# Eight units on the input without its root, in three places of a two-layer transformer trunk

## The reference, cut to what is computed

```python
def _rms(x, g):
    xf = x.astype(jnp.float32)
    y = xf * lax.rsqrt(jnp.mean(xf * xf, axis=-1, keepdims=True) + EPS)
    return (y * g.astype(jnp.float32)).astype(x.dtype)
...
def _layer(x, cond, p, lam_init, pos, ctx):
    mod = jnp.einsum('bd,de->be', jax.nn.silu(cond), p['w_ada']) + p['b_ada']
    sh1, sc1, g1, sh2, sc2, g2 = jnp.split(mod[:, None, :], 6, axis=-1)
    h = _rms(x, p['g_norm1']) * (1 + sc1) + sh1
    u = h @ p['w_in']
    gates, xa, qkv_da, xc, mla_in = jnp.split(u, IN_SPLITS, axis=-1)
    ...
    merged = jnp.sum(gsig * proj, axis=2)
    x = x + g1 * (merged @ p['w_out'])
    h2 = _rms(x, p['g_norm2']) * (1 + sc2) + sh2
    x = x + g2 * _conv_ffn(h2, p['w_up'], p['conv_w'], p['conv_b'], p['w_down'])
```

## Time and profile before

| | |
|---|---|
| three runs | 1223.28, 1224.08, 1226.67 us, median 1224.08 |
| profiled execution, its own time | 1223.51 us |
| its span, first to last instruction | 1221.7 us |
| PE busy | 99 % of the span, 7816 matmuls |
| DVE busy | 74 % |
| ACT busy | 47 % |
| POOL busy | 11 % |
| chain that ended last | PE 93 %, DVE 2 %, POOL 2 %, DMA 1 %, issue 1 % |

### The profile page before, as it was taken

How to read it: one execution, slowest core, us unless ns; L and a number is a source line. 1 busy time by engine, 2 the same in 40 slices (tenths; PEclk the granted TensorE clock), 3 DMA queues, 4 the chain that set the end, 5 groups by cost and what they waited for, 6 DMA issues and landing times.

```text
span 1221.7 us, 19781 instructions
## 1 busy us (share of the span) xinstructions
PE 1208.0 (99%) x7816; PEld 1149.7 (94%) x7816; DVE 901.4 (74%) x1671; ACT 575.6 (47%) x949; POOL 136.8 (11%) x109
## 2 busy tenths in 40 slices
PE   8999999999999999999999999999999999999998
PEld 7987999989989999999989889999998999999998
DVE  5597877748689999986876965765686887887432
ACT  3445564643365544532354455645425554454321
POOL 0232000008300000000202500000271000000000
PEclk9999999999999999999999999999999999999999
DMA  9763433444744444469664522332345334334443
GB/s 370 291 220 125 147 117 112 172 139 161 253 173 144 167 156 159 169 216 322 214 234 163 189 87 87 104 104 87 104 167 196 122 124 135 122 123 136 134 142 121
DMA packets 53532, 198.82 MB, mean 163 GB/s; under 512 B 6784, under 2 KB 7200, under 8 KB 51904
## 3 DMA queue, kind: packets, MB, share of 16 engines
q1 hardware_dynamic: 53120, 196.86, 46.0%
q0 software_dynamic: 320, 0.69, 0.2%
HBM read 195.25 MB, written 2.27 MB: 162 GB/s over the span
## 4 chain that ended last, share of the span: by engine, by line
PE 93%; DVE 2%; POOL 2%; DMA 1%; issue 1%; ACT 0%; SPq 0%; DVEq 0%; POOLq 0%; ACTq 0%
PE bank L1444 27%; PE bank L1446 27%; PE bank L1445 26%; PE bank L1743 1%; PE bank L1723 1%; PE bank L1512 1%; DVE w_lo L980 1%; DMA start_ada<-start_ada 1%; PE bank L1517 1%; PE bank L1516 1%; POOL wide L653 1%; PE bank L1713 1%; POOL merge_sum L655 1%; PE bank L1501 1%; PE bank L1698 1%
## 5 line engine op out<-in xcount | busy, mean ns | idle before, releaser
L1444 PE MATMUL bank<-act_hi,w_hi 128*128 128x384 f32 x1368 | 465.0, 340 | 0.7 <-DVE act_lo L1055 0.3
L1446 PE MATMUL bank<-act_hi,w_lo 128*128 128x384 f32 x1368 | 457.8, 335 | 0.0
L1445 PE MATMUL bank<-act_lo,w_hi 128*128 128x384 f32 x1336 | 446.6, 334 | 0.0
L980 DVE TENSOR_TENSOR w_lo<-w_raw,w_hi 128x1024 fp32r<-128x1024 f32 x251 | 318.9, 1272 | 114.6 <-ACT w_hi L662 113.6
L662 ACT ACTIVATE w_hi<-w_raw 128x1024 fp32r<-128x1024 f32 x251 | 264.3, 1054 | 167.8 <-DMA w_raw<-stream 167.7
L1444 PEld LDWEIGHTS bank<-act_hi,w_hi 128*128 128x128 f32 x1368 | 257.1, 188 | 10.7 <-issue 6.5
L1446 PEld LDWEIGHTS bank<-act_hi,w_lo 128*128 128x128 f32 x1368 | 256.8, 188 | 0.0
L1445 PEld LDWEIGHTS bank<-act_lo,w_hi 128*128 128x128 f32 x1336 | 251.0, 188 | 0.6
L1446 PE MATMUL bank<-mlp_hi,w_lo 128*128 128x384 f32 x352 | 118.3, 336 | 0.0
L1444 PE MATMUL bank<-mlp_hi,w_hi 128*128 128x384 f32 x352 | 118.3, 336 | 0.0
L1445 PE MATMUL bank<-mlp_lo,w_hi 128*128 128x384 f32 x352 | 118.3, 336 | 0.0
(11 more groups left out here) (246 smaller groups left out, 1576.0 us busy)
## 6 DMA issues: line engine op xcount, KB each, us to landing
w_raw<-stream SPq DMA_DIRECT2D x251, 512.0 KB, 3.3
ada<-ada_rows SPq DMA_DIRECT2D x48, 512.0 KB, 4.4
start_ada<-start_ada SPq DMA_DIRECT2D x8, 1024.0 KB, 17.9
ada_norm<-ada_w SPq DMA_DIRECT2D x16, 512.0 KB, 5.8
ada<-ada_w SPq DMA_DIRECT2D x8, 512.0 KB, 5.5
start_raw<-start_w SPq DMA_DIRECT2D x8, 448.0 KB, 18.5
ada_head_a<-ada_w SPq DMA_DIRECT2D x5, 512.0 KB, 7.3
cond_spread_mix<-cond_rows SPq DMA_DIRECT2D x2, 1024.0 KB, 7.9
```

What stands on the lines that cost most here:

```text
L980: V.tensor_tensor(wlo[s][:, :], raw[s][:, :], whi[s][:, :].bitcast(F32), ALU.subtract).then_inc(lo_ready, 1)
L1444: T.matmul(out, wb[s][0][:, w, :], hi[k], start=first and k == 0, stop=False)
L1445: T.matmul(out, wb[s][0][:, w, :], lo[k], start=False, stop=False)
L1446: ins = T.matmul(out, wb[s][1][:, w, :], hi[k], start=False, stop=last and k == n - 1)
```

## The change

It does three things of one kind, and moves what they displace.

1. **Start (layer 0).** The seven units and an eighth are multiplied with x·scale, without the root; two more columns carry the shift of the two conditionings, so the matmuls have 386 columns. Behind the products DVE multiplies each bank by the root (`start_rescale`) and ACT adds the shift's product (`start_add_shift`). The root is made in the middle of the loop (`roots(0)` at j = 4). The normalised x, which the later units need, is made meanwhile: POOL x·scale·root, ACT plus shift, DVE the low rest, at the blocks that `START_NORMED` names. x is loaded in four quarters between the weights, the modulation weights have three buffers (six before), and PE's warm-up has 6 products (11 before).
2. **Second mixing stage (layer 1).** `first_units(0, ...)`: units 0 to 7 on the unnormalised x, 386 columns, the sum of squares between blocks 4 and 5 of the first unit. ACT and DVE prepare the unnormalised high and low part during the down stage of layer 0.
3. **Second up stage (layer 1).** The same with `first_units(1, ...)`: the first eight up units go to eight banks, are rescaled in place, and then pass the convolution.

`hole_units` and the second `norm_units` are gone with their loads; the modulation vectors (1,3) and (1,5) are made by DVE's row products instead: layer 1 has the `MIX_ROWS` and `STEP_ROWS` of layer 0 (32 products where there were 16), and 16 more from the fourth group of four up units on (`SLOW_ROWS`). In the down stage of layer 0 the 26 row products lie at other units (`DOWN_ROWS`) and read a vector loaded anew (`spread_down`, 1 MB). The mixing units change order: xc0 and xc1 before k0 and k1.

The diff, cut:

```diff
-START_ADA = 6
-WARM = 11
+START_ADA = 3
+WARM = 6
+START_UNITS = SKIP + 1
+START_NORMED = {4: (0,), 5: (1, 2), 6: (3, 4), 7: (5, 6)}
...
+FIRST = 8
+SLOW_ROWS = 3
...
@@ POOL @@
+                def normed(n):
+                    pool.wait_ge(rstd_ready, l * 2 + n + 1)
+                    for k in range(KD):
+                        nc.gpsimd.tensor_tensor(wide[:, k, :], late[:, k, :], rsn, ALU.mult).then_inc(norm_full, 1)
...
+                    pool.wait_ge(rstd_ready, 1)
+                    for k in range(KD):
+                        pool.wait_ge(start_full, k + 1)
+                        nc.gpsimd.tensor_tensor(wide[:, k, :], late[:, k, :], rsn, ALU.mult).then_inc(norm_full, 1)
...
@@ ACT @@
+                def unnormed_high(n, d):
+                    for a, e, c in RANGES:
+                        ins = A(late[:, d, a:e], x[:, d, a:e], ACT.Copy, scale=(sc1, sc2)[n][:, d, c:c + 1])
+                    ins.then_inc(u_full, 1)
+                    act.wait_ge(u_full, n * KD + d + 1)
+                    A(uhi[n][:, d, 0:TOK], late[:, d, :], ACT.Copy).then_inc(u_hi, 1)
...
                 if l == 0:
-                    for u in range(SKIP, SKIP + 3):
-                        split(u)
+                    for j in range(KD):
+                        if j < KD // 2:
+                            start_square(j)
+                        start_high(j)
+                        if j == KD // 2:
+                            roots(0)
+                        start_unnormed_high(j)
+                        for k in START_NORMED.get(j, ()):
+                            normed_high(0, k)
+                    split(SKIP)
+                    normed_high(0, KD - 1)
+                    split(SKIP + 1)
+                    for q in range(START_UNITS):
+                        start_add_shift(q)
+                        if q == 2:
+                            split(SKIP + 2)
+                        if MIX[q] in SQUARED:
+                            mix_squares(q)
...
@@ DVE @@
+                def rescale(n, q, out):
+                    u = (0, P0)[n] + q
+                    dve.wait_ge(rstd_ready, l * 2 + n + 1)
+                    dve.wait_ge(unit_done, FROM + l * UNITS + u + 1)
+                    b = bank[q % (4, 8)[n]]
+                    V.tensor_copy(sums_shift[:, q, :], b[:, TOK:wide_w])
+                    V.tensor_tensor(out, b[:, 0:TOK], rsn, ALU.mult).then_inc(rescaled, 1)
...
+                    start_low(j)
+                    dve.wait_ge(start_u_hi, j + 1)
+                    low(sulo[:, j, 0:TOK], late[:, j, :], suhi[:, j, 0:TOK])
+                    low(sulo[:, j, TOK:start_width], mod[:, j, :], suhi[:, j, TOK:start_width]).then_inc(start_u_lo, 1)
...
                     for j in range(KD):
-                        start_norm(j)
-                    for u in range(SKIP, SKIP + 3):
-                        split(u)
+                        start_unnormed_low(j)
+                        for k in START_NORMED.get(j, ()):
+                            normed_low(0, k)
+                    split(SKIP)
+                    normed_low(0, KD - 1)
+                    split(SKIP + 1)
+                    for q in range(START_UNITS):
+                        start_rescale(q)
+                        if q == 2:
+                            split(SKIP + 2)
...
@@ DVE, up pairs @@
+                        unnormed = l > 0 and i < 2
+                        first, b0 = 3 * (2 * i + j), up_bank(i, 2 * j)
+                        if unnormed and p > l * FB:
+                            split(u + 4, i)
+                        elif not unnormed and (l == 0 or i > 2 or j > 0):
+                            split(u + 3, i)
...
+                        if unnormed and first < KD:
+                            normed_low(1, first)
                         dve.wait_ge(mlp_tanh, p + 1)
...
+                        if unnormed and first + 1 < KD:
+                            normed_low(1, first + 1)
+                        split(u + (5 if unnormed else 4), i)
+                        if unnormed and b0 < FIRST - 2:
+                            rescale(1, b0 + 2, bank[b0 + 2][:, 0:TOK])
...
+                        if unnormed and b0 < FIRST - 2:
+                            rescale(1, b0 + 3, bank[b0 + 3][:, 0:TOK])
+                        if unnormed and first + 2 < KD:
+                            normed_low(1, first + 2)
...
@@ PE @@
+                def first_units(n, u0, ready, counts):
+                    for q in range(FIRST):
+                        unit_ready(u0 + q)
+                        if q < 4:
+                            pe.wait_ge(ready, counts[q])
+                        elif n == 0:
+                            pe.wait_ge(mix_out, l * U_MIX + q - 3)
+                        else:
+                            pe.wait_ge(rstd_ready, l * 2 + n + 1)
+                        out = bank[q % (4, 8)[n]][:, 0:wide_w]
+                        for k in range(KD):
+                            if q == 0:
+                                pe.wait_ge(u_lo, n * (KD + 1) + k + 1 + (n == 1 or k >= 3))
+                            ins = dense(out, u0 + q, [k], [uhi[n][:, k, :]], [ulo[n][:, k, :]], k == 0, k == KD - 1)
+                            if q == 0 and k == 4:
+                                square_sums(n)
+                        ins.then_inc(unit_done, 1)
...
                     for j in range(KD):
-                        start_products(j)
-                        if j + 2 < KD:
-                            start_modulate(j + 2)
+                        if 1 <= j < KD - 1:
+                            start_modulate(j + 1)
+                        start_high_products(j)
+                        if j == 0:
+                            start_modulate(1)
+                        if j == KD // 2 - 1:
+                            start_squares()
+                        start_low_products(j)
...
-                    square_sums(0)
-                    hole_units()
-                    group(0, (0, 1, 2), HI, LO, lambda k: pe.wait_ge(norm_lo, l * 2 * KD + k + 1))
+                    first_units(0, 0, x2_ready, [FROM + KD // 2 + 1 + q for q in range(4)])
```

More of the change, by code:

```diff
@@ L708, in rstds, with roots @@
                             after[i]()
-                def norm(n):
-                    shift = mod[:, 0:8, :] if n == 0 else mod[:, 24:32, :]
+                def roots(n):
                     act.wait_ge(ss_done, l * 2 + n + 1)
-                    own(A(rsn, bank[SUM_BANK[n]][:, 0:TOK], ACT.Ln, scale=1.0 / D, bias=EPSC))
+                    sums = bank[SUM_BANK[n + (l and n)]][:, 0:TOK] if l + n else bank[7][:, P:P + TOK]
+                    own(A(rsn, sums, ACT.Ln, scale=1.0 / D, bias=EPSC))
@@ L741, in _ @@
+                for u in range(FIRST, U_MIX):
+                    split(u + 2)
                     if u == U_MIX - 4:
@@ L1330, in _ @@
                             modulation(0, 4)
+                            own(scales(sc2, 32, "g2"))
                         else:
                             row_bias(1, 4)
-                        scales(sc2, 32, "g2")
-                split(P0 + 2)
-                norm(1)
-                modulation(l, 5)
+                            scales(sc2, 32, "g2").then_inc(scale_ready, 1)
+                            row_bias(1, 3)
+                            unnormed_shift_low(1)
+                    elif l > 0:
+                        unnormed_low(1, d - 1)
+                if l > 0:
+                    unnormed_low(1, KD - 1)
+                split(P0 + 2)
+                if l == 0:
+                    norm(1)
+                    modulation(l, 5)
+                else:
+                    split(P0 + 3)
+                    for q in range(2):
+                        rescale(1, q, bank[q][:, 0:TOK])
                 for i in range(FB // 2):
```

476 lines of the change are left out of this document (295 added, 181 removed).

## The result

The changed kernel takes 1229.29 us (median of 7 runs, 1228.24 to 1230.65) against 1223.28 (median of 7): ratio 1.0044, 95 % interval 1.0033 to 1.0055. The profiled execution took 1228.24 us, its span is 1226.4 us; those of before are 1223.51 and 1221.7, so the two traces differ by 4.7 us.

The account below looks back on a forecast made before the run. PE, busy 99 % of the span, was taken to bound the kernel; 1223.51 - 4.5 (second mixing stage) - 3.0 (second up stage) + 3.8 (start) = 1219.8 us, range 1215.3 to 1224.5.

Parts of the forecast that it names:

- Start, +3.8 forecast: Layer 0's start: values begin at 60.5 and not at 56.71, 3.8 us lost; bounds 0.6 and 5.0 lost.
- M: In the start: the end of the fifth modulation product on PE, forecast at 29.6.
- contention: In the start: DVE's rests with SBUF inputs and POOL's products wait for each other, 3.2 us of the loss.
- PE's own work behind M: In the start: the same 22.0 us as before, the sums taking the place of small gaps.
- the chain of the hand-over: Before layer 0's values: unit 9's split comes behind normalised blocks, splits and shifts, so PE waits 2.7 us.
- Second mixing stage, 4.5 forecast: Layer 1's first seam: 6.31 - 2.0 - 0.16, and 0.3 for a stall that goes: 4.5 us gained, bounds 3.5 and 4.8.
- tightest place: Second mixing stage: the values unit wants unit 6 handed over when unit 7 ends, slack 0.3.
- Second up stage, 3.0 forecast: Layer 1's up seam: it shrinks by 4.0 us, 1.0 is lost again: 3.0 gained, bounds 1.0 and 4.0.
- stall at unit 12: Second up stage: DVE falls behind, unit 12 wanted at 52.05, ready at 52.65; 1.0 us charged, bounds 0 and 3.
- Rival B: Second up stage: POOL's products and DVE's operations lengthen the overloaded first three pairs, 8.6 us more, 1228.4; chance 0.08.
- upper end of the range: Whole kernel: 1224.5, given as the forecast with the start fully blocked and the up stage at its bound.
- Rival D: 386-column matmuls, rows 1544 bytes apart, run slower; 7 ns each on 576 would take the whole gain; chance 0.03.

Follow-up runs that it names:

- the kernel with the old start: Changed kernel with the start of the kernel before, new order only at layer 1's two seams, shared area where it lay before: 1218.46 us, ratio 0.9954.
- the repair: Against the 1218.46 us kernel: at the second mixing stage ScalarE splits unit u+4 before shifting unit u; unnormalised tiles also re-placed: 1216.44 us, ratio 0.9940.
- the last run: Against the 1216.44 us kernel: the two shift columns left out of layer 1's 384 unnormalised matmuls, tiles and distances kept: 1216.57 us (one run).
- the five later versions: Changed kernel without the 64 bytes, 1225.18 us; also split earlier and old warm-up, 1221.20; old start, 1218.46; that with repairs, 1216.44; without the two columns, 1216.57.

## Why the prediction was wrong

1219.8 was forecast and 1228.24 came, in the profiled execution. The 8.4 us between them, by the steps of the sum:

- **Not in the sum: place of the tiles, 4.2 us.** The unused 64 bytes alone make the trace 4.2 us longer (span 1225.9 against 1221.7). By stages of that trace it is 1.41 and 1.40 (down), 0.25 and 0.06 (out), 0.56 and 0.45 (branch), and next to nothing elsewhere. The prediction took the price of a matmul from one stretch of before and charged the untouched stages nothing. I read the diff for what it computes and not for what it moves in memory. This alone takes back the whole gain of 3.7 us that was forecast. It is the step that failed most; but without it the kernel still is 1.1 us slower than before, not faster, so the steps below failed too.
- **Start, +3.8 forecast, 4.57 at the first value unit.** The price behind M was right as a total, 30.9 forecast and 31.1 measured, but by luck, for its reasons were shared out wrongly: contention 3.2 forecast and 1.75 measured by taking the products away; PE's own work behind M was put at no more than before, and is 0.9 more (22.9 without the products against 22.0), for the sum of squares and the longer 386-column matmuls; the chain of the hand-over made PE wait 3.4 and not 2.7. M came at 30.2 and not at 29.6, still before the 30.54 of the old order; that 0.6 is within what M differs by between traces.
- **Not in the sum: the clock behind the wait, 1.55 us.** The forecast had the hole, 2 to 3 us, but charged only its length.
- **Second mixing stage, 4.5 forecast, 3.1 gained.** The "tightest place" had a slack of 0.3 and came out 1.1 us late; the same wait, 0.93 in the kernel with the old start, went to nothing by the repair. The other part is the columns: 3.3 ns in each of 192 matmuls are 0.63, where 0.0005 to 0.0009 us each, 0.16 at most, had been charged by a rate per column. The sums gave 0.4 back: 1.6 us (631.70 to 633.34) and not 2.0.
- **Second up stage, 3.0 forecast, 3.7 gained.** No stall at unit 12: PE is busy for all of 185.73 us. DVE's taps of the first pair start 12.3 us behind the last out matmul, 12.0 forecast. The 1.0 charged for that stall was not paid, and the sums took 1.6 and not 2.0; the longer matmuls of 386 columns took 0.5 more than charged. As the last run shows, it is they that hide the stall. Rival B's backlog did not come.
- **Not in the sum: layer 1's out stage, 0.4.** It takes 36.28 us, and 36.28 to 36.48 in the five later versions with the new seams and the shared area in its old place, against 35.83 before and 35.89 with only the 64 bytes. So it comes with the new seams, for which ACT and DVE make unnormalised parts in this stage. PE has a new gap of 0.17 us at 927.56; what ended it the profile does not show.
- **A conditioning load in layer 0's branch stage, about 0.6.** At its last one PE waits 1.17 us, and 0.66 in the kernel before. No run was made for it, and it may be chance: with 128 and 192 unused bytes and every load as before, PE waits 1.5 and 1.4 us there.

4.2, 0.8, 1.55, 1.4, -0.7, 0.4 and 0.6 make 8.25 of the 8.44. The added row products cost nothing, as forecast: the stretch from layer 1's values to its out stage has 26.8 us more of DVE (164.32 to 191.10) and 0.58 more of time, nearly all of which its branch matmuls lost (0.45). The upper end of the range, 1224.5, does not follow from the terms given for it: start at its bound and up stage at its bound make 1223.51 - 4.5 - 1.0 + 5.0 = 1223.0. Rival D had the right suspicion, that a changed layout makes a matmul slower, but looked for it only in the new tiles, priced them at 7 ns and gave it 0.03; the new tiles lose 3.3 ns, and the old ones behind the inserted tile 2.5 to 3. The rule on exclusion of the Trainium skill (page "SBUF — State Buffer", section "Who interferes with whom") holds in these traces for operations of two columns, but it would not have saved the forecast: the sum by that rule was 1221.0.

## What to carry to other kernels

When PE is busy 99 % of the time, the start-to-start time of an untouched stage is the first thing to compare: equal counts with a longer stretch mean that the matmul itself changed. A new tile is a change to every address behind it; put it at the end, or pad it so that streamed and weight tiles keep their remainders by 256. A hole in PE costs its length and, at 3.56 us here though not at 2.32, a slow clock behind it; before moving work into a chain, look whether the chain's last link (here a split queued behind hand-overs) could go first.

## What the runs showed of the hardware

- A dense matmul of 384 columns starts 173.2 to 174.5 ns behind the last one (means of stages), and 175.8 to 176.2 where its streamed tile and its weight tile lie on a multiple of 256 and 128 bytes behind one, whichever is which (the kernels with 64 bytes ahead of the shared area and with 128 ahead of the weights). Both on one, both 128 behind, or 64 or 192 apart: fast.
- Two more columns than 384 cost 3.3 ns a matmul, 173.4 to 176.7, where 0.5 % of the columns would be 0.9.
- Beside GpSimd's products of 384 columns, an operation of VectorE with two inputs in SBUF waits even when it has two columns: 0.97 us against 0.15 without the products.
- Behind a wait of PE of 3.56 us from start to start the granted clock was 0.83 over the next 10 us, 1.55 us lost; behind one of 2.32 us it stayed at 1.00.
